# Memory attention in a decoder trunk: query and output weights multiplied with the memory's keys and values on chip

## The chip, the cores and the metric

The kernel runs on one core of a Trainium2 chip. The metric is the device time of one execution in microseconds (us), and lower is better. Engines are named as in the profile: PE is TensorE's matrix unit (PEld its weight load), DVE is VectorE, ACT is ScalarE, POOL is GpSimd, SP is SyncE, which here only starts DMA transfers.

## The reference, cut to what matters

One layer is applied to a prompt of 2048 tokens and to 8 separate decode tokens. A mixer (a gated convolution beside an mLSTM with 4 heads) is followed by attention over 256 memory rows and a SwiGLU feed-forward part; all of it is fp32. What the change touches is the attention:

```python
def mem_kv(mem, g_mem, w_xkv):
    kk, vv = jnp.split(rmsnorm(mem, g_mem) @ w_xkv, 2, axis=-1)
...
def cross_attn(xn, mk, mv, w_xq, w_xo):
    q = (xn @ w_xq).reshape(B, T, X_HEADS, X_HEAD_DIM)      # 4 heads of 256
    s = jnp.einsum('bthd,bmhd->bhtm', q, mk) * (X_HEAD_DIM ** -0.5)
    p = jax.nn.softmax(s, axis=-1)
    o = jnp.einsum('bhtm,bmhd->bthd', p, mv).reshape(B, T, X_HEADS * X_HEAD_DIM)
    return o @ w_xo
...
hp = hp + cross_attn(rmsnorm(hp, g_cross), pk, pv, w_xq, w_xo)             # prompt: its own memory
hs = hs + cross_attn(rmsnorm(hs, g_cross), cache_mem_k, cache_mem_v, ...)  # decode: cached keys, values
```

The memory keys and values of the prompt (pk, pv) are outputs as well.

## The kernel before

**Blocks.** The prompt is cut into five blocks of 4, 3, 3, 3 and 3 chunks of 128 tokens (`BLK`), that is one block 512 tokens wide and four 384 wide. The 8 decode tokens ride as 8 more columns: through the mixer with block 1 (`DM`), through the output projection and the query projection with block 2 (`DO`), through attention's output projection and the feed-forward part with block 3 (`DX`).

**Groups.** All weights are cut into groups of [128, 1024], that is 8 tiles of 128x128. `gemm` (L487) runs one group: for each of the 8 tiles three matmuls, since each fp32 operand is split in a high and a low part (hi x hi, hi x lo, lo x hi), with the weights stationary and the tokens moving; all of them stand on line 503. First come 16 groups for the memory's keys and values (`G_KV`), 256 columns wide. Then each block has 121 groups: 1 for the gates, 4 for `sg`, 24 for the heads of the mixer, 8 for its output (OUT), 8 for the queries (XQ), 8 for attention's output (XO), and 68 for the feed-forward part in three rounds. A stage can be found in the trace by counting matmuls of line 503: 24 make a group (fewer in the last two rounds of the feed-forward part), 384 the memory's part, 2856 a block.

**Weights.** A group's split weights lie in one of `NS` = 5 slots of `w_hl`. In block 0 a group comes from HBM as raw fp32 into one of two `w_raw` buffers, ACT makes the high part (`w_high`, L812), POOL the low part (L407; DVE does it for the 16 groups of the memory, L1164), and SP stores both to `split_d` in HBM (`keep`, 1 MB). In the later blocks SP loads the 1 MB of the split group (`split`, L344) as soon as the slot's last user is done. SP's queue is in order.

**Attention, before.** After `opening` (L653), which runs two XQ groups and a sum of squares for the norm, the XQ groups go on; DVE scales each result by the norm (`query`, L1441), ACT and DVE split it in high and low. Between the gemm steps, by hooks at fixed places, PE runs per head: `scores` (L662; 6 matmuls of 256 columns for each chunk, line 671), `ptrans` (L676; transposes of the probabilities, line 681) and `pv` (L684; 4 plain fp32 products as wide as the block, line 688). DVE takes maxima and normalises, ACT exponentiates, and both move results between them. The XO groups run interleaved with the last two heads. Plain fp32 products stand in the trace as two matmul records each.

**Around it.** In the mixer's heads PE runs per chunk `t_part` (transposes, keys by queries) and `n_part` (products with the state) from hooks between gemm steps, each at a place of its own. In block 0, `turn_mem` transposes the memory's values (16 transposes, line 537) in the `sg` stage. Decode attention runs on DVE in the feed-forward part of block 2 in 32 pieces (`dec_piece`) at the places of `PIECE_AT`; their rows and caches are loaded from POOL's queue (`decode_caches`). PE has `NP` = 3 banks for gemm results, so it can be two groups ahead of the engine that reads them.

## Time and profile before

| | us |
|---|---|
| median of 3 runs | 2981.76 (2981.4 to 2985.2) |
| the profiled execution, its own time | 2983.26 |
| its span, first to last instruction | 2981.4 |
| PE busy in the span | 2932.7 (98%) |
| DVE, ACT, POOL busy | 1212.0, 762.6, 378.2 |
| memory's 16 groups (9.09 to 73.55) | 64.46 |
| XQ and XO of block 0 (317.01 to 437.71) | 120.70 |
| XQ and XO of block 4 (2603.07 to 2692.61) | 89.54 |

Matmuls overlap in the pipeline, so the mean length of one record is longer than the time from one start to the next; a stage's own length, divided by its matmuls, gives that time. A time of a stretch holds waits as well as work. The mean granted clock of TensorE is 0.995 of full speed, and the DMA engines move 260 GB/s on average.

### The profile page before, as it was taken

What the parts mean: (1) busy time and instruction counts of PE and PEld (TensorE: products, weight loads), DVE (VectorE), ACT (ScalarE), POOL (GpSimd) and SP (SyncE); (2) the same over time, 40 slices, a digit from 0 to 9 for tenths busy, and PEclk for the clock granted to TensorE, in tenths of its full rate; (3) what the DMA queues carried; (4) which work ended last, traced back from release to release, by engine and by line L of the source; (5) the groups of instructions that cost most, each with busy time, mean ns of one, the idle gap of its engine ahead of it and who ended that gap; (6) DMA issues with size and microseconds to landing.
All of it is one profiled execution on the core that took longest, in us unless ns stands there. A gap on an engine that the chain in (4) does not pass through costs nothing.

```text
span 2981.4 us, 39316 instructions
## 1 busy us (share of the span) xinstructions
PE 2932.7 (98%) x16212; PEld 2771.1 (93%) x16212; DVE 1212.0 (41%) x2327; ACT 762.6 (26%) x1510; POOL 378.2 (13%) x251
## 2 busy tenths in 40 slices
PE   7999999999999999999999999999999999999998
PEld 7778778888899999999999999999999999999998
DVE  6355554234624344233344546334322243442223
ACT  4433433232332220113232011322311032231001
POOL 0443434444210000000000111000000000000000
PEclk9999999999999999999999999999999999999999
DMA  5876858789776498777667989866467777647775
GB/s 198 318 261 221 281 199 302 267 283 317 283 279 245 159 328 301 267 265 282 216 227 269 339 323 370 304 225 251 170 242 260 261 258 274 227 176 250 254 268 193
DMA packets 126873, 776.11 MB, mean 260 GB/s; under 512 B 15172, under 2 KB 18692, under 8 KB 46952
## 3 DMA queue, kind: packets, MB, share of 16 engines
q1 hardware_dynamic: 109840, 710.78, 65.7%
q0 software_dynamic: 13904, 59.48, 5.9%
q10 hardware_dynamic: 2952, 3.34, 0.4%
q8 instruction: 130, 2.13, 0.3%
q14 instruction: 47, 0.39, 0.0%
HBM read 633.59 MB, written 139.95 MB: 259 GB/s over the span
## 4 chain that ended last, share of the span: by engine, by line
PE 89%; DMA 4%; DVE 2%; ACT 2%; POOL 1%; issue 1%; SPq 0%; ACTq 0%; DVEq 0%
PE gb L503 82%; DMA w_raw<-w_st 2%; PE ta L671 2%; POOL w_hl L407 1%; DMA w_hl<-split_d 1%; PE tb L688 1%; PE td L688 1%; ACT w_hl L812 1%; DMA w_raw<-w_kv 1%; PE ta L592 0%; DVE w_hl L1164 0%; PE ta L511 0%; PE tb L561 0%; PE gm L681 0%; PE tb L603 0%
## 5 line engine op out<-in xcount | busy, mean ns | idle before, releaser
L503 PE MATMUL gb<-xn_hi,w_hl 128*128 128x384 f32 (+2 forms) x6480 | 1795.7, 351 | 10.7 <-DVE xn_lo L1159 4.3
L503 PEld LDWEIGHTS gb<-xn_hi,w_hl 128*128 128x128 f32 x6480 | 1188.5, 188 | 70.8 <-DMA w_hl<-split_d 5.8
L503 PE MATMUL gb<-xn_lo,w_hl 128*128 128x384 f32 (+2 forms) x3240 | 1124.3, 347 | 0.0
L503 PE MATMUL gb<-act_hi,w_hl 128*128 128x384 f32 (+3 forms) x3296 | 874.3, 344 | 17.3 <-DVE w_hl L1164 10.7
L503 PEld LDWEIGHTS gb<-act_hi,w_hl 128*128 128x128 f32 x3296 | 599.3, 189 | 44.9 <-DVE w_hl L1164 11.0
L503 PEld LDWEIGHTS gb<-xn_lo,w_hl 128*128 128x128 f32 x3240 | 610.4, 188 | 29.0 <-issue 1.4
L503 PE MATMUL gb<-act_lo,w_hl 128*128 128x384 f32 (+3 forms) x1648 | 564.1, 342 | 0.0
L1207 DVE TENSOR_TENSOR work<-gb,r_res 128x384 f32<-128x384 f32 (+2 forms) x260 | 151.7, 585 | 633.4 <-PE gb L503 570.4
L407 POOL TENSOR_TENSOR w_hl<-w_raw,w_hl 128x1024 fp32r<-128x1024 f32 x121 | 294.6, 2439 | 484.8 <-ACT w_hl L812 484.8
L503 PEld LDWEIGHTS gb<-act_lo,w_hl 128*128 128x128 f32 x1648 | 311.9, 189 | 13.4 <-issue 0.7
L1393 DVE TENSOR_TENSOR x<-x,gb 128x384 f32<-128x384 f32 (+2 forms) x200 | 115.3, 581 | 374.6 <-PE gb L503 371.9
L812 ACT ACTIVATE w_hl<-w_raw 128x1024 fp32r<-128x1024 f32 x132 | 138.9, 1057 | 323.5 <-DMA w_raw<-w_st 160.4
L1069 ACT ACTIVATE work<-work 128x384 f32<-128x384 f32 (+2 forms) x110 | 59.9, 545 | 504.6 <-DVE work L1207 504.5
L1072 ACT ACTIVATE act_hi<-work 128x384 fp32r<-128x384 f32 (+2 forms) x110 | 60.0, 546 | 345.5 <-DVE work L1620 345.5
L986 ACT ACTIVATE work<-x 128x384 f32<-128x384 f32 (+2 forms) x120 | 65.5, 546 | 270.1 <-DVE x L1393 249.8
L1403 DVE TENSOR_TENSOR r_res<-r_res,work 128x384 f32<-128x384 f32 (+2 forms) x120 | 94.6, 788 | 69.2 <-ACT work L986 67.7
L1620 DVE TENSOR_TENSOR work<-work 128x384 f32<-128x384 f32 (+2 forms) x110 | 86.6, 787 | 30.7 <-ACT work L1069 20.5
L876 ACT ACTIVATE big<-gb,cst 128x384 f32<-128x384 f32 (+1 forms) x80 | 48.6, 608 | 197.0 <-PE gb L503 196.8
L378 POOL DMA_DIRECT2D big<-rows_d x20 | 10.9, 550 | 684.4 <-DMA rows_d<-big 684.4
L1607 DVE TENSOR_TENSOR act_lo<-work,act_hi 128x384 fp32r<-128x384 f32 (+2 forms) x110 | 85.6, 778 | 14.5 <-ACT act_hi L1072 13.9
L1303 DVE TENSOR_TENSOR work<-ta,big 128x128 f32<-128x128 f32 x64 | 18.6, 291 | 150.4 <-ACT work L957 150.4
L1406 DVE SCALAR_TENSOR_TENSOR xn_lo<-x,cst,xn_hi 128x384 fp32r<-128x384 f32 (+2 forms) x80 | 55.8, 697 | 0.0
(246 smaller groups left out, 1809.0 us busy)
## 6 DMA issues: line engine op xcount, KB each, us to landing
w_hl<-split_d SPq DMA_DIRECT2D x484, 1024.0 KB, 5.1
split_d<-w_hl SPq DMA_DIRECT2D x121, 1024.0 KB, 5.0
w_raw<-w_st SPq DMA_DIRECT2D x121, 512.0 KB, 5.9
w_raw<-w_kv SPq DMA_DIRECT2D x16, 512.0 KB, 3.4
big<-kd_d POOLq DMA_DIRECT2D x8, 1024.0 KB, 8.4
big<-vd_d POOLq DMA_DIRECT2D x8, 1024.0 KB, 11.4
x<-x_blk POOLq DMA_DIRECT2D x8, 768.0 KB, 8.9
big<-x_blk POOLq DMA_DIRECT2D x6, 768.0 KB, 6.1
```

The costliest lines, as they stand in the source:

```text
L407: pool.tensor_tensor(w_lo[:, g % NS, :], w_raw[:, g % NR, :], w_hi[:, g % NS, :].bitcast(F32), ALU.subtract).then_inc(w_lo_done, 1)
L503: mm = pe.matmul(gb[:, ps, 0:wd], a[:, s, k * P:(k + 1) * P], r[:, k, 0:wd], start=(first and k == ks[0] and i == 0), stop=(last and k == ...
L671: mm = pe.matmul(ta[:, t // 2, (t % 2) * 256:(t % 2) * 256 + 256], a[:, kt, t * P:(t + 1) * P], r[:, kt, :], start=(dt == 0 and i == 0), s ...
L812: act.activation(w_hi[:, n % NS, :], w_raw[:, n % NR, :], ACT.Copy).then_inc(w_hi_done, 1)
L986: act.activation(sq_res[:, 0:wd], x[:, e, 0:wd], ACT.Square).then_inc(res_sq, 1)
L1069: act.activation(et[:, 0:W], gt[:, 0:W], ACT.Silu).then_inc(e_ffn, 1)
L1072: act.activation(act_hi[:, f, 0:W], ht[:, 0:W], ACT.Copy).then_inc(hid_hi, 1)
L1207: return lambda ps: v.tensor_tensor(dst[:, 0:wd], ps[:, 0:wd], r_res[:, 0:wd], ALU.mult)
L1393: return lambda ps: v.tensor_tensor(x[:, e, 0:wd], x[:, e, 0:wd], ps[:, 0:wd], ALU.add)
L1403: v.tensor_tensor(acc_res[:, 0:wd], acc_res[:, 0:wd], sq_res[:, 0:wd], ALU.add).then_inc(res_acc, 1)
L1607: v.tensor_tensor(act_lo[:, f, 0:W], ht[:, 0:W], act_hi[:, f, 0:W].bitcast(F32), ALU.subtract).then_inc(hid_lo, 1)
L1620: v.tensor_tensor(ht[:, 0:W], et[:, 0:W], ut[:, 0:W], ALU.mult).then_inc(h_ffn, 1)
```

## The change

For each head, scores are xn (Wq Kt), and the attention's output is P (V Wo). The change makes both products once, after the memory's groups, and stores them into `split_d` at the places of the XQ and XO groups, which then hold 1024 x 1024 products instead of weights:

- 32 products (`NPRE`): 16 for the keys (12 matmuls of 256 columns each), 16 for the values (6 of 512). ACT and DVE split each in high and low into a ring of four buffers (`made`), and ACT stores it in two DMA transfers. The weights come as 16 more raw groups (`G_MEM` = 16, `G_KV` = 32). The norm of block 0's input (`next_scale`, `next_high`, `next_low`) moves from the memory's groups into this stage.
- In every block, XQ becomes `wide`: tokens are stationary, the product moves with 512 columns, and the scores of two heads for a chunk come out by token in one bank. The norm is one number per token and is applied in the exponent's scale. `scores`, `pv`, `query` and the copies between them go; XO runs on the probabilities' transposes. Groups of XQ and XO are not loaded raw in block 0 but as split groups, by a loop on SP.
- The decode tokens no longer ride in XQ and XO. Their query and output projections are plain fp32 products of 8 stationary columns and 512 moving ones: 16 between the XO groups of block 2 (`decode_queries`), 16 between the OUT groups of block 3 (`decode_outputs`), with rows of `w_xq` and `w_xo` loaded from POOL's queue (`decode_rows`), and 8 small transposes.
- `NS` is 6. `turn_mem` goes. In the heads, `t_part` and `n_part` share hooks. The 32 pieces of decode attention keep their number and start two places later.

```diff
-G_KV = 16
+G_MEM = 16
+G_KV = 32
+NPRE = 32
-NS = 5
+NS = 6
-PIECE_AT = [2 * f + 1 for f in range(1, 8)] + [16 + m for m in (0, 1, 2, 4, 5, 6)] + [G1 + 2 * f + 1 for f in range(3)]
+PIECE_AT = [2 * f + 1 for f in range(3, 8)] + [16 + m for m in range(8)] + [G1 + 2 * f + 1 for f in range(3)]
...
+def raw(g):
+    return g < G_LOW and not attends(g)
...
-        mem_k_hi = sb("mem_k_hi", [P, KT, NMEM], F32R)
-        mem_k_lo = sb("mem_k_lo", [P, KT, NMEM], F32R)
-        mem_v = sb("mem_v", [P, MT, D])
+        dwt = sb("dwt", [P, 4, D])
...
+                if g == gw(0, O_OUT + KT - 1):
+                    for made_stored in pre_stored:
+                        sp.wait_ge(made_stored, 8 * NPRE)
+                    for a in range(gw(0, O_XQ), gw(0, O_FF[0])):
+                        kept(sp, a - NS)
+                        split(a)
...
+            def decode_rows(i):
+                after(pool, dw_used, i - 3)
+                pool.dma_start(dwt[:, i % 4, :], w_dec[i] if i < KT else w_kv[G_MEM + i]).then_inc(dw_loaded[i % 4], 16)
...
+            for h in range(HEADS):
+                pe.wait_ge(mem_lo, 2 * h + 2)
+                for j in range(4):
+                    i = h * 4 + j
+                    bank = pre_bank(i)
+                    for n in range(2):
+                        for dt in range(2):
+                            g = G_MEM + 2 * h + dt
+                            if j == 0 and n == 0:
+                                slot_ready(g)
+                            c = (2 * j + n) * P
+                            for f, (a, r) in enumerate([(w_hi, act_hi), (w_hi, act_lo), (w_lo, act_hi)]):
+                                mm = pe.matmul(bank[:, n * NMEM:(n + 1) * NMEM], a[:, g % NS, c:c + P], r[:, 2 * h + dt, NMEM:2 * NMEM],
+                                               start=(dt == 0 and f == 0), stop=(dt == 1 and f == 2))
+                    if j < 3:
+                        mm.then_inc(pre_done, 1)
+                    else:
+                        mm.then_inc(group_done, 2)
+            for h in range(HEADS):
+                pe.wait_ge(mem_lo, KT + 2 * h + 2)
+                for j in range(4):
+                    i = HEADS * 4 + h * 4 + j
+                    bank = pre_bank(i)
+                    mt, half = j // 2, j % 2
+                    for dt in range(2):
+                        g = G_MEM + KT + 2 * h + dt
+                        if j == 0:
+                            slot_ready(g)
+                        for f, (a, r) in enumerate([(act_hi, w_hi), (act_lo, w_hi), (act_hi, w_lo)]):
+                            mm = pe.matmul(bank, a[:, 2 * h + dt, mt * P:(mt + 1) * P], r[:, g % NS, half * 512:half * 512 + 512],
+                                           start=(dt == 0 and f == 0), stop=(dt == 1 and f == 2))
+                    if j < 3:
+                        mm.then_inc(pre_done, 1)
+                    else:
+                        mm.then_inc(group_done, 2)
...
-                    if b == 0:
-                        hooks[6] = lambda: turn_mem(h)
...
+                    c_hooks = {2: lambda: t_part(h, 0), 6: lambda: t_part(h, 1) or n_part(h, 0)}
                     if CH == 3:
-                        c_hooks = {2: lambda: t_part(h, 0), 4: lambda: t_part(h, 1), 7: lambda: n_part(h, 0)}
-                        h_hooks = {1: lambda: t_part(h, 2), 3: lambda: n_part(h, 1), 7: lambda: n_part(h, 2)}
+                        h_hooks = {2: lambda: t_part(h, 2) or n_part(h, 1), 7: lambda: n_part(h, 2)}
                         b_hooks = None
                     else:
-                        c_hooks = {2: lambda: t_part(h, 0), 4: lambda: t_part(h, 1), 6: lambda: n_part(h, 0)}
-                        h_hooks = {0: lambda: t_part(h, 2), 2: lambda: n_part(h, 1), 4: lambda: t_part(h, 3), 6: lambda: n_part(h, 2)}
+                        h_hooks = {1: lambda: t_part(h, 2) or n_part(h, 1), 5: lambda: t_part(h, 3) or n_part(h, 2)}
                         b_hooks = {1: lambda: n_part(h, 3)}
...
+                def decode_outputs(m):
+                    if m == 3:
+                        pe.wait_ge(do_ready, 2 * NDEC)
+                    for i in (2 * (m - 3), 2 * (m - 3) + 1):
+                        pe.wait_ge(dw_loaded[i % 4], 16 * ((KT + i) // 4) + 16)
+                        for half, bank in enumerate((ta[:, 1, :], td)):
+                            mm = pe.matmul(bank[0:NDEC, :], dy[:, i * NDEC:(i + 1) * NDEC], dwt[:, i % 4, half * 512:half * 512 + 512],
+                                           start=i == 0, stop=i == KT - 1)
+                        mm.then_inc(dw_used, 1)
+                def turn_outputs():
+                    pe.wait_ge(qrow_done, 4)
+                    for i in range(KT):
+                        mm = pe.matmul(tb[:, i * NDEC:(i + 1) * NDEC], dwt[0:NDEC, 0, i * P:(i + 1) * P], ident[0:NDEC, 0:NDEC],
+                                       start=True, stop=True)
+                    mm.then_inc(dox_t, 1)
...
+                def sum_cols():
+                    pe.wait_ge(res_acc, b * 27 + 9)
                     for t in range(CH):
-                        for dt in range(2):
-                            kt = 2 * h + dt
-                            for i, (a, r) in enumerate([(act_hi, mem_k_hi), (act_lo, mem_k_hi), (act_hi, mem_k_lo)]):
-                                mm = pe.matmul(ta[:, t // 2, (t % 2) * 256:(t % 2) * 256 + 256], a[:, kt, t * P:(t + 1) * P],
-                                               r[:, kt, :], start=(dt == 0 and i == 0), stop=(dt == 1 and i == 2))
-                        if t % 2 or t == CH - 1:
...
+                def wide(p, hooks):
+                    for q in range(4):
+                        g = gw(b, O_XQ) + 4 * p + q
+                        slot_ready(g)
                         for t in range(CH):
-                            m = pe.transpose(bank[:, t * P:(t + 1) * P], prob[:, t, mt * P:(mt + 1) * P], ident)
-                        m.then_inc(pt_done, 1)
+                            for n in range(2):
+                                kt = 2 * q + n
+                                if p == 0 and t == 0:
+                                    pe.wait_ge(res_lo, b * 16 + kt + 1)
+                                for f, (a, r) in enumerate([(xn_hi, w_hi), (xn_lo, w_hi), (xn_hi, w_lo)]):
+                                    mm = pe.matmul(score_bank(p, t), a[:, kt, t * P:(t + 1) * P], r[:, g % NS, n * 512:n * 512 + 512],
+                                                   start=(kt == 0 and f == 0), stop=(kt == KT - 1 and f == 2))
+                            if t == CH - 1:
+                                mm.then_inc(group_done, 1)
+                            elif q == 3:
+                                mm.then_inc(s_done, 1)
+                            if (q, t) in hooks:
+                                hooks[q, t]()
+                wide(0, {(1, CH - 1): sum_cols})
+                    wide(1, {(1, 2): lambda: ptrans(0, 0) or ptrans(0, 1), (2, 2): lambda: ptrans(1, 0) or ptrans(1, 1)})
...
+                def decode_queries(m):
+                    if m == 3:
+                        pe.wait_ge(dxq_ready, 1)
+                        pe.wait_ge(exp_done, ch0(b + 1))
+                    for i in (2 * (m - 3), 2 * (m - 3) + 1):
+                        decode_product(i, i, dxq[:, i, :], (ta[:, 1, :], td))
...
-                    gemm(gw(b, O_XO + i), W, act_hi, act_lo, (2 * h, 2 * h + 1), None if i else o_wait,
+                    gemm(gw(b, O_XO + i), TOK, act_hi, act_lo, (2 * h, 2 * h + 1), None if i else o_wait,
                          first=h == 0, last=h == HEADS - 1)
                 xo(0, 0)
-                ptrans(2)
                 xo(1, 0)
-                scores(3)
                 xo(2, 0)
-                pv(2)
                 xo(0, 1)
+                ptrans(2, 0)
+                ptrans(2, 1)
                 xo(1, 1)
-                ptrans(3)
-                xo(0, 2)
-                xo(1, 2)
-                pv(3)
                 xo(2, 1)
-                xo(2, 2)
-                for i in range(3):
-                    xo(i, 3)
+                ptrans(3, 0)
+                ptrans(3, 1)
+                for h in (2, 3):
+                    for i in range(3):
+                        xo(i, h)
...
+            def store_made(i):
+                act.wait_ge(pre_lo, i + 1)
+                h, j = (i // 4) % HEADS, i % 4
+                for s in range(2):
+                    if i < NPRE // 2:
+                        dst = split_d[O_XQ + 4 * (h // 2) + j, :, s, :].rearrange("p (n h m) -> p n h m", n=2, h=2)[:, :, h % 2, :]
+                        act.dma_start(dst, made[:, i % 4, s, :].rearrange("p (n m) -> p n m", n=2)).then_inc(pre_stored[i % 4], 16)
+                    else:
+                        kt, m0 = 2 * h + j // 2, O_XO + j % 2 * 4
+                        dst = split_d[m0:m0 + 4, :, s, kt * P:(kt + 1) * P].rearrange("m p c -> p m c")
+                        act.dma_start(dst, made[:, i % 4, s, :].rearrange("p (m c) -> p m c", m=4)).then_inc(pre_stored[i % 4], 16)
+            for i in range(NPRE):
+                pre_made(act, i)
+                after(act, pre_stored[i % 4], 32 * (i // 4))
+                act.activation(made[:, i % 4, 0, :].bitcast(F32R), gb[:, (G_MEM + i) % NP, :], ACT.Copy).then_inc(pre_hi, 1)
+                if i:
+                    store_made(i - 1)
+                if i % 4 == 3:
+                    w_high(G_MEM + i // 4 * 2)
+                    w_high(G_MEM + i // 4 * 2 + 1)
+                if i < KT:
+                    read_out(act, G_MEM - 1)
+                    act.activation(act_hi[:, i, 0:NMEM], vfeat[:, i, :], ACT.Copy).then_inc(mem_hi, 1)
+                elif i < 2 * KT:
+                    next_high(0, i - KT)
+            store_made(NPRE - 1)
...
+            for i in range(NPRE):
+                v.wait_ge(pre_hi, i + 1)
+                v.tensor_tensor(made[:, i % 4, 1, :].bitcast(F32R), gb[:, (G_MEM + i) % NP, :], made[:, i % 4, 0, :],
+                                ALU.subtract).then_inc(pre_lo, 1)
+                if i < KT:
+                    v.wait_ge(mem_hi, KT + i + 1)
+                    v.tensor_tensor(act_lo[:, i, 0:NMEM], vfeat[:, i, :], act_hi[:, i, 0:NMEM].bitcast(F32),
+                                    ALU.subtract).then_inc(mem_lo, 1)
+                    next_scale(0, i)
+                elif i < 2 * KT:
+                    next_low(0, i - KT)
...
+                def maxima(p, t):
+                    if t < CH - 1:
+                        v.wait_ge(s_done, ch0(b) // 2 - 2 * b + p * (CH - 1) + t + 1)
+                    else:
+                        v.wait_ge(group_done, gw(b, O_XQ) + 4 * p + 4)
+                    st(v.tensor_reduce(mx[:, t, :, 0], score_bank(p, t).rearrange("p (h m) -> p h m", h=2), AX.X, ALU.max))
+                    st.settle()
+                    v.tensor_scalar(mx[:, t, :, 1], mx[:, t, :, 0], r_neg[:, t:t + 1], None, ALU.mult).then_inc(mx_done, 1)
+                def normalise(p, t):
+                    v.wait_ge(exp_done, ch0(b, 2 * p) + 2 * t + 2)
+                    st(v.reciprocal(mx[:, t, :, 3], mx[:, t, :, 2]))
+                    st.settle()
+                    for i in range(2):
+                        v.tensor_scalar(prob[:, t, i, :], prob[:, t, i, :], mx[:, t, i, 3:4], None, ALU.mult).then_inc(p_done, 1)
+                for p in range(2):
+                    maxima(p, 0)
+                    for t in range(1, CH):
+                        maxima(p, t)
+                        normalise(p, t - 1)
+                    normalise(p, CH - 1)
+                    prob_low(2 * p)
+                    prob_low(2 * p + 1)
```

## Rows read from the trace of the kernel before

**Rows 1.** The page, part 1: PE's busy time, share of the span, instructions.
```profile
PE 2932.7 (98%) x16212; PEld 2771.1 (93%) x16212; DVE 1212.0 (41%) x2327; ACT 762.6 (26%) x1510; POOL 378.2 (13%) x251
```

**Rows 2.** The chain in order of time: start us, length us, what, instructions.
```profile
385.61 2.87 PE ta L671 x24
...
449.34 161.88 PE gb L503 x714
...
2700.70 267.32 PE gb L503 x1542
```

**Rows 3.** Stretches: from:to, length, each engine's busy us, clock, DMA share, GB/s.
```profile
9.09:73.55 64.46, 54.41 (x389) 51.44 (x389) 46.34 (x67) 33.12 (x50) 5.57 (x2) 0.95 0.57 189
73.55:86.27 12.72, 8.42 (x25) 6.05 (x25) 8.73 (x11) 5.83 (x11) 5.08 (x3) 0.78 0.92 347
86.27:112.94 26.67, 26.67 (x116) 21.54 (x115) 11.55 (x14) 11.70 (x19) 12.01 (x5) 0.91 0.88 323
...
317.01:381.82 64.81, 62.38 (x299) 49.57 (x298) 36.06 (x61) 27.25 (x54) 22.98 (x11) 1.00 0.77 266
381.82:437.71 55.89, 55.37 (x250) 43.53 (x248) 29.52 (x38) 21.24 (x36) 17.22 (x7) 1.00 0.49 174
...
2603.07:2649.97 46.90, 46.90 (x278) 44.44 (x278) 19.57 (x51) 13.96 (x37) 0.00 (x0) 1.00 0.49 181
2649.97:2692.61 42.64, 42.17 (x239) 39.70 (x239) 17.97 (x38) 12.94 (x29) 0.00 (x0) 1.00 0.53 195
...
1793.34:1856.61 63.27, 60.55 (x336) 58.06 (x337) 45.67 (x67) 6.84 (x13) 7.91 (x12) 1.00 1.01 393
```

**Rows 4.** Timeline, PE: start, length, what; plain fp32 products, 512 columns.
```profile
375.66 1.88 PE L688 MATMUL td<-big,mem_v 128*128 128x512 f32 x4
377.37 1.88 PE L688 MATMUL tb<-big,mem_v 128*128 128x512 f32 x4
```

**Rows 5.** Timeline, PE: the first two gemm matmuls behind an `n_part`.
```profile
901.23 0.43 PE L503 MATMUL gb<-xn_hi,w_hl 128*128 128x392 f32 x1
901.49 0.35 PE L503 MATMUL gb<-xn_lo,w_hl 128*128 128x392 f32 x1
```

**Rows 6.** Groups by form, ACT: busy us, mean ns, idle before and its releasers.
```profile
L812 ACT ACTIVATE w_hl<-w_raw 128x1024 fp32r<-128x1024 f32 x132 | 138.9, 1057 | 323.5 <-DMA w_raw<-w_st 160.4 <-issue 111.4 <-PE gb L503 46.1
...
L829 ACT ACTIVATE xn_hi<-big 128x512 fp32r<-128x512 f32 x8 | 5.0, 629 | 9.3 <-DVE big L1153 9.3
...
L1012 ACT ACTIVATE act_hi<-tb 128x512 fp32r<-128x512 f32 x4 | 2.4, 600 | 4.5 <-PE tb L688 4.5
```

**Rows 7.** Timeline, ACT: its sequencer starting one DMA transfer.
```profile
28.03 0.45 ACTq L847 DMA_DIRECT2D dec<-st_m  x1
```

**Rows 8.** Waits of ACT from 66 to 440 us: total us, times, longest.
```profile
ACT w_hl L812 <- DMA w_raw<-w_st: 37.7, 16, 4.4
```

**Rows 9.** One stretch, columns as in group 3; SP's and ACT's queues both move.
```profile
20.00:28.00 8.00, 6.52 (x36) 6.17 (x36) 4.37 (x9) 3.67 (x10) 0.00 (x0) 0.63 0.92 351
```

**Rows 10.** DMA issues: queue, count, KB each, median us to landing.
```profile
x<-mem_x ACTq DMA_DIRECT2D x4, 256.0 KB, 7.9
...
o_mv<-work SPq DMA_DIRECT2D x1, 1024.0 KB, 9.6
```

**Rows 11.** Groups by form, the softmax on ACT and DVE.
```profile
L1000 ACT ACTIVATE work<-ta,work 128x256 f32<-128x256 f32 x64 | 29.6, 471 | 48.7 <-DVE work L1425 48.7
...
L1000 ACT ACTIVATION_READ_ACCUMULATOR work<-ta,work 128x1 f32 x64 | 12.8, 200 | 0.0
...
L1433 DVE TENSOR_SCALAR work<-work 128x256 f32<-128x256 f32 x64 | 22.6, 354 | 2.3
...
L1422 DVE TENSOR_REDUCE work<-ta 128x2 f32<-128x512 f32 x24 | 16.6, 690 | 24.9 <-PE ta L671 24.9
```

**Rows 12.** Groups by form: POOL's low parts; DVE reading a 512-column bank.
```profile
L407 POOL TENSOR_TENSOR w_hl<-w_raw,w_hl 128x1024 fp32r<-128x1024 f32 x121 | 294.6, 2439 | 484.8 <-ACT w_hl L812 484.8
...
L1207 DVE TENSOR_TENSOR work<-gb,r_res 128x512 f32<-128x512 f32 x52 | 35.8, 689 | 117.6 <-PE gb L503 111.2 <-ACT r_res L819 6.4
```

453 lines of the change are left out of this document (232 added, 221 removed).

## The prediction

> **What bounds the kernel now.** I read the page first: PE is busy for 98% of the span and no other engine for half of it [rows 1]. So only PE's time counts, as work or as gaps, and I cost every edit there. The chain in order of time gives PE's prices, because long runs of one line have no gap in them: 714 matmuls of 512 columns in 161.88 us are 226.7 ns each, 1542 of 384 in 267.32 are 173.4, 24 score matmuls of 256 in 2.87 are 119.6 [rows 2]. I then cut the span by counting matmuls of line 503 and read the stretches. Attention takes 89.5 us in block 4 and 120.7 in block 0 [rows 3]; the pairs of blocks 1, 2 and 3 are three more like block 4's, within 0.8 us. Of 89.5 us, 384 gemm matmuls are 66.6. The first stretches are the other place to look: the memory's groups take 64.5 us with PE busy for 54.4, the gate group behind them 12.7 us, and there the clock and the DMA share (0.92) show a stage that isn't PE's alone [rows 3].
>
> **Attention, blocks 1 to 4.** Scores go: 72 matmuls at 119.6 ns, 8.6 us. The products with the values go: two plain fp32 products of 512 columns start 1.71 us apart from the next two [rows 4], so one is 857 ns; at 384 columns it is 643, and 16 are 10.3 us. XQ's 192 matmuls of 384 columns (33.3 us) become 144 of 512 (32.6): 0.7 less. XO and the transposes stay. Each change from small products back to gemm costs 0.26 us where 0.177 is usual [rows 5], some 0.085 more; thirteen insertions become five, 0.7 less. New is one wait. The softmax of the second pair of heads starts when `wide(1)` ends, and PE has only four XO pieces (24 matmuls, 4.2 us) to cover it. Its last chunk needs a maximum 0.7, two exponents with their sums 2 x 0.67, two scalings 2 x 0.35 [rows 11], and about 1.7 for the normalising of the chunk before it, small operations and signals (an estimate): 4.5 us. So 0.4 us stays open; the first pair has 8.2 us of `wide(1)` over it and costs nothing. Sum: 8.6 + 10.3 + 0.7 + 0.7 - 0.4 = 19.9 us a block, **79.6** for four.
>
> **Attention, block 0.** Scores 96 x 119.6 = 11.5, values 16 x 857 = 13.7, insertions 0.7. Besides, of 120.7 us about 116.6 are work by the same prices, and of the 4 us of gaps I let 2.8 go, since its groups come split and ACT and POOL no longer have to split them in time. **28.7**.
>
> **The new stage.** PE needs 16 x 12 x 119.6 + 16 x 6 x 226.7 ns = 44.7 us, but it isn't PE that sets it. ACT does, per product, a copy out of the bank (600 ns) and two DMA starts (450 each) [rows 6, 7], and over the stage 16 weight copies of 1057 ns and 16 further copies of up to 629 [rows 6]: 19.2 + 28.8 + 16.9 + 10.1 = 75 us. DVE has 32 x 0.69 and the moved norm, POOL 16 x 2.44 = 39 us [rows 12]; both are under that. DMA moves 16.8 MB of products, 5.2 MB of weights and, behind them on SP's queue, some 6.3 MB of the next groups; at 351 GB/s for a share of 0.92 [rows 9] that is 74 us. Two engines so evenly loaded don't overlap fully: ACT waits for a raw weight, and all products queue behind it. Block 0 shows 16 such waits of 2.4 us [rows 8]; ten weights are still to come, and I let seven or eight of them wait: 18. I take 75 + 18 = 93 us. The bounds: 74 if nothing waits; above, the ring of four buffers. A product's buffer is free when its store has landed, issued one product later, so a period of (landing + 1.5) / 3. ACT's 256 KB loads at the start landed in 7.9 us, a 1 MB store in 9.6 [rows 10]: 3.1 to 3.7 us a product, 100 to 118 us. The memory's groups lose the moved norm (3 us of gaps by the stretch's end), and the gate group finds its weights and its norm ready: 6 us for 12.7. From 9.09 to the end of the gate group that is 61.4 + 93 + 6 = 160.4 for 77.2: **83.2 more**.
>
> At TensorE's lower clock level (1.2 GHz, not 2.4), which the stretch around the start shows after PE had waited there (0.63 mean [rows 9]), the 32 products would take PE 89 us, still under 93. So the clock doesn't set this stage; it can add up to 5 us to the gate group behind it, and that is in the range.
>
> **The other parts.** `sg`: 26.7 us [rows 3] less 21.8 for its 96 matmuls and 0.9 for the picked row leave 4.0 for `turn_mem` and the lower clock: **4.0** gained. Shared hooks: two insertions fewer per head and 384-wide block, three in block 0, at 0.085: 3.7, less a doubt about new waits for DVE: **3.5**. Decode: 32 plain products of 512 columns at 857 ns, 27.4, and 1.6 for eight small transposes and ACT's copies in front of them: **29.0 more**; the 8 columns saved in XQ and XO are 0.6 and disappear in it. Its rows, 4 MB twice from POOL's queue, I cost at nothing: a row is asked for when its buffer is free and used two groups and three products later (some 10 us or more). If that cover is gone, PE stands for the rest of a landing, a few us in two blocks. The later pieces of decode attention cost nothing while PE can be two groups ahead. The sixth slot: in block 2's third feed-forward round 14 groups of 24 took 63.3 us where 336 x 173.4 ns is 58.3, with the DMA engines at a share of 1.01 [rows 3]; one more slot is 1 MB of lead, and I give it 3 of the 5 us, **3.0**. Its other effect, that each block's attention no longer gives DMA a rest (0.49 and 0.53 of the engines there, [rows 3]), I cost at nothing: the feed-forward groups ask the same rate without gaps.
>
> **Sum.** +83.2 - 4.0 - 3.5 - 28.7 - 79.6 + 29.0 - 3.0 = -6.6 us. The profiled execution took 2983.26 with a span of 2981.4, the median of three is 2981.76, so span and median are the same to 0.4 us and I take the sum from the median: **2975 us**.
>
> **The rivals.**
> 1. *The new stage runs at ACT's own pace.* Stores land early and weights are there: 74 us and not 93, 2956 us. For it: six weights are split ahead, and the 16 last products carry no norm. Against it: the shares of ACT and DMA, 75 and 74 us, leave no room. A rule stands on its side: the Trainium skill, DMA: Bandwidth & Descriptors, section "Anatomy of one DMA — SWDGE (gpsimd) path", gives about 2 us plus the bytes at 436 GB/s for one transfer (fitted for transfers from GpSimd). An estimate by it is 2.6 us for 256 KB, a ring that never waits, and so this rival's 2956; the 7.9 us of the row speak against it, and no row shows such a store alone. 0.22.
> 2. *The ring of stores sets the stage: slower.* Once a store takes longer than 7.2 us to land, the period passes the 2.9 us of my 93. At 9.6 it is 118, the whole 3000 us. For it: the landings seen, and pieces of 512 bytes to 1 KB. Against it: those landings were queued behind larger ones. 0.20.
> 3. *The softmax isn't covered.* PE has one place per block where nothing else can go. If ACT and DVE take 9 us and not 4.5, each block gives 5 back: 25 us, 3000. Against it: the waits before, with shorter covers, were 0.5 us. 0.08.
>
> **How the numbers follow.** My case has 0.50, with a range of 2964 to 2986 of its own. The range of 8 in 10 reaches into the rivals: 2952 to 3000. A measurement of this kernel can tell about 0.2%, 6 us, so "faster" is under 2976 and "slower" over 2988. Faster: about half of my case and all of rival 1, 0.48. Same: the rest of my case below 2988 and the mild end of rival 2, 0.25. Slower: 0.27.
>
> **What would show it.** Right: block 4's attention at 69 to 70 us; 72 records of scores and 32 of values gone; block 0's at 92; a stretch of about 93 us between the last memory group and the gate group in which ACT is busy for most of the time, counting its DMA starts, and waits for raw weights; OUT of block 3 and XO of block 2 longer by 14 us each; block 2's third round near 60. Wrong: a stage under 80 or over 105 us; PE waiting for probabilities by more than 1 us a block; plain products of 8 rows at another price than 857 ns; gaps of PE behind DMA in blocks 1 to 4, which would mean that the rest in attention was needed; heads longer than before.

## The result, and the profile after

| | before | after |
|---|---|---|
| median of 5 runs, us | 2981.76 (2979.66 to 2985.2) | 2999.5 (2996.88 to 3001.9) |
| the profiled execution, its span, us | 2981.4 | 2999.2 |
| mean granted clock | 0.995 | 0.991 |

The changed kernel is slower by 17.7 us: the ratio is 1.0058, with a 95% interval of 1.0045 to 1.007. The forecast was 2975, within 2952 to 3000, and "slower" had a chance of 0.27. PE is less busy than before by 15 us, against [rows 1], in a span that is 18 us longer. So the change removed work from PE, as forecast, and put more than twice as much waiting in its place.

The page of the changed kernel, part 1:

```profile
PE 2917.5 (97%) x15851; PEld 2728.0 (91%) x15851; DVE 1171.4 (39%) x2249; ACT 745.1 (25%) x1470; POOL 386.3 (13%) x267
```

The stages were cut by counting gemm matmuls, as for [rows 3], with the same columns (from:to, length, busy us of PE, PEld, DVE, ACT, POOL, clock, DMA share, GB/s). In order: the memory's groups, the products of the keys, those of the values, the gate group, `sg`, block 0's heads; block 0's scores and XO; block 2's XO, its second and third feed-forward rounds; block 3's OUT; block 4's scores and XO.

```profile
9.33:77.05 67.72, 55.87 (x389) 53.07 (x389) 42.27 (x58) 32.73 (x50) 7.21 (x3) 1.00 0.55 178
77.05:122.23 45.18, 28.75 (x193) 27.01 (x193) 36.57 (x41) 22.69 (x40) 22.05 (x9) 0.89 0.76 255
122.23:168.56 46.33, 29.66 (x96) 21.31 (x97) 14.36 (x22) 18.73 (x27) 19.29 (x8) 0.81 1.02 324
168.56:175.67 7.11, 7.11 (x25) 5.73 (x25) 0.93 (x2) 1.06 (x1) 1.39 (x1) 0.77 1.02 379
175.67:198.33 22.66, 22.66 (x100) 18.40 (x98) 5.60 (x10) 6.83 (x10) 8.20 (x4) 1.00 0.96 356
198.33:369.67 171.34, 160.85 (x774) 134.38 (x772) 75.22 (x143) 67.23 (x131) 64.63 (x31) 0.96 0.73 258
413.65:459.95 46.30, 46.30 (x217) 38.50 (x216) 12.70 (x32) 9.19 (x25) 0.00 (x0) 1.00 0.52 183
459.95:506.29 46.34, 45.57 (x209) 37.62 (x208) 29.74 (x44) 20.19 (x39) 12.44 (x5) 1.00 0.59 212
1596.09:1645.72 49.63, 49.63 (x237) 36.98 (x236) 16.94 (x36) 11.20 (x26) 3.18 (x6) 1.00 0.68 254
1746.54:1808.62 62.08, 59.68 (x342) 58.74 (x341) 29.59 (x43) 10.96 (x19) 4.43 (x7) 1.00 0.84 320
1837.74:1897.66 59.92, 59.17 (x338) 58.08 (x337) 44.95 (x67) 6.83 (x13) 10.03 (x16) 1.00 1.02 401
2065.65:2116.34 50.69, 50.69 (x244) 37.81 (x244) 15.79 (x30) 9.23 (x18) 3.65 (x6) 1.00 0.66 239
2640.49:2675.23 34.74, 34.74 (x163) 28.92 (x163) 10.91 (x30) 8.22 (x25) 0.00 (x0) 1.00 0.69 244
2675.23:2709.90 34.67, 34.67 (x206) 34.59 (x205) 16.95 (x36) 11.22 (x26) 0.00 (x0) 1.00 0.65 239
```

Most of the forecast stands here as it was made: block 4's attention takes 69.4 us, block 0's 92.6, the products 91.5. The row to look at is the sixth. It is a stage whose weights and products the change doesn't touch; I had only let it gain a little by the shared hooks. Before, it was this, in the kernel before, same view:

```profile
112.94:273.02 160.08, 155.87 (x773) 130.06 (x772) 76.02 (x143) 63.06 (x126) 60.07 (x29) 0.99 0.74 260
```

It is 11.3 us longer, PE is idle for 10.5 us in it (4.2 before), and its clock is 0.96. The table sets each term of the sum beside what was measured (stage after less stage before, in us; a minus is a gain).

| term | forecast | measured |
|---|---|---|
| memory's groups | -3.1 | +3.3 |
| the products | +93 | +91.5 |
| gate group | -6.7 | -5.6 |
| `sg` | -4.0 | -4.0 |
| heads, all blocks | -3.5 | +11.4 |
| attention, block 0 | -28.7 | -28.1 |
| attention, blocks 1 to 4 | -79.6 | -81.7 |
| decode products | +29.0 | +32.0 |
| sixth slot, block 2's third round | -3.0 | -3.4 |
| later pieces, block 2's second round | 0 | +2.9 |
| sum | -6.6 | +18.3 |

The difference to +17.7 lies in small changes of other stages. The forecast missed by 24.3 us: 14.9 of it in the heads, 6.4 in the memory's groups, 3.0 in the decode products, 2.9 in the pieces; the other stages give 2.9 back. The waits of PE in block 0's heads (engine, tile and line waited for: us, times, longest), in the kernel before and then in the changed one, and the changed kernel's clock there, in stretches of 6 us:

```profile
PE tb L603 <- DVE work L1304: 4.2, 3, 2.1
```
```profile
PE tb L708 <- DVE work L1498: 6.3, 4, 2.4
PE tb L672 <- ACT big L1106: 4.2, 1, 4.2
```
```profile
204.30:210.30 6.00, 3.98 (x13) 3.53 (x14) 0.00 (x0) 4.39 (x7) 1.38 (x3) 0.64 0.57 187
210.30:216.30 6.00, 6.00 (x20) 5.02 (x19) 1.13 (x2) 4.45 (x4) 5.63 (x4) 0.51 0.89 306
216.30:222.30 6.00, 6.00 (x28) 4.95 (x27) 0.20 (x1) 1.75 (x2) 1.19 (x1) 1.00 0.92 345
```

PE stands for 4.2 us (to 206.3), and then TensorE runs at its lower level (1.2 GHz, 0.51 of the 2.4) until 216: of the PE time in the first two of these stretches, 3.98 x 0.36 + 6.00 x 0.49 = 4.4 us are lost to that, by this estimate. With 4.2 for the wait and 2.1 for longer waits at line 708 (6.3, at line 603 before 4.2) this is 10.7 of the 11.3. What PE waits for is the exponents of the gates' rows. ACT's timeline (start, length, what, idle before it):

```profile
203.94 1.06 ACT L969 ACTIVATE w_hl<-w_raw 128x1024 fp32r<-128x1024 f32 x1 [4.02 <-issue]
204.90 0.61 ACT L1101 ACTIVATE big<-big 128x512 f32<-128x512 f32 x1
...
206.06 0.21 ACT L1106 ACTIVATE big<-big 128x4 f32<-128x4 f32 x1
```

By DVE's timeline their input was ready at 193.3. They ran at 204.9: ACT's queue is in order, and three weight copies of block 0 stand ahead of them, which ACT reached at 194.3, 198.3 and 203.9 after standing for 6.1, 2.4 and 4.0 us. By the program each waits for its turn in the loop of load, high part, low part and store. My theory was that the opening leaves ACT's queue behind in that loop. The rivals were the shared hooks, and a plain lack of DMA bandwidth.

### The profile page after: what moved, and what is told of

Read it like the earlier page. It is cut to its first block, busy times and chain, and to the rows that moved or that the text cites. A ratio compares the mean times of both kernels' runs of the same rounds, so it can differ in the third digit from the quotient of the medians.

```text
span 2999.2 us, 38561 instructions
## 1 busy us (share of the span) xinstructions
PE 2917.5 (97%) x15851; PEld 2728.0 (91%) x15851; DVE 1171.4 (39%) x2249; ACT 745.1 (25%) x1470; POOL 386.3 (13%) x267
## 4 chain that ended last, share of the span: by engine, by line
PE 87%; DMA 5%; DVE 2%; ACT 2%; POOL 1%; issue 1%; ACTq 1%; SPq 0%; DVEq 0%
PE gb L580 76%; PE gb L828 3%; DMA w_raw<-w_st 2%; PE ta L828 2%; DMA w_raw<-w_kv 1%; POOL w_hl L460 1%; ACT w_hl L969 1%; PE td L828 1%; DMA big<-kd_d 1%; ACTq L1048 1%; DMA w_hl<-split_d 1%; PE ta L697 0%; PE gm L810 0%; PE tb L708 0%; DVE work L1498 0%
## 5 line engine op out<-in xcount | busy, mean ns | idle before, releaser
L580 PE MATMUL gb<-xn_hi,w_hl 128*128 128x384 f32 (+2 forms) x5840 | 1598.7, 350 | 5.3 <-issue 2.2
L580 PEld LDWEIGHTS gb<-xn_hi,w_hl 128*128 128x128 f32 x5840 | 1070.7, 188 | 56.4 <-issue 6.6
L580 PE MATMUL gb<-xn_lo,w_hl 128*128 128x384 f32 (+2 forms) x2920 | 1013.5, 347 | 0.0
L580 PE MATMUL gb<-act_hi,w_hl 128*128 128x384 f32 (+3 forms) x3296 | 872.2, 344 | 20.9 <-DVE w_hl L1352 11.3
L580 PEld LDWEIGHTS gb<-xn_lo,w_hl 128*128 128x128 f32 x2920 | 550.0, 188 | 25.3 <-issue 0.7
L1402 DVE TENSOR_TENSOR work<-gb,r_res 128x384 f32<-128x384 f32 (+2 forms) x220 | 128.3, 585 | 554.6 <-PE gb L580 518.4
L1599 DVE TENSOR_TENSOR r_res<-r_res,work 128x384 f32<-128x384 f32 (+2 forms) x120 | 81.4, 678 | 56.5 <-ACT work L1187 54.9
L429 POOL DMA_DIRECT2D big<-rows_d x20 | 10.9, 552 | 667.5 <-DMA rows_d<-big 667.5
L828 PE MATMUL gb<-w_hl,xn_hi 128*128 128x512 f32 x240 | 76.5, 392 | 0.0
```

The costliest lines, as they stand in the source:

```text
L580: mm = pe.matmul(gb[:, ps, 0:wd], a[:, s, k * P:(k + 1) * P], r[:, k, 0:wd], start=(first and k == ks[0] and i == 0), stop=(last and k == ...
L828: mm = pe.matmul(score_bank(p, t), a[:, kt, t * P:(t + 1) * P], r[:, g % NS, n * 512:n * 512 + 512], start=(kt == 0 and f == 0), stop=(kt ...
L1402: return lambda ps: v.tensor_tensor(dst[:, 0:wd], ps[:, 0:wd], r_res[:, 0:wd], ALU.mult)
L1599: v.tensor_tensor(acc_res[:, 0:wd], acc_res[:, 0:wd], sq_res[:, 0:wd], ALU.add).then_inc(res_acc, 1)
```

## The experiments

Each run is compared with runs of the kernel before on the same chip. Stages are cut as above, and a ratio without more words is to the kernel before.

**The order of ACT's queue.**

```diff
-                for h in range(HEADS):
-                    if h == HEADS - 1:
+                def row_exps():
                         act.wait_ge(rows_pre, b + 1)
                         st(act.activation(row_g[:, 0:TOK], row_g[:, 0:TOK], ACT.Exp))
...
+                for h in range(HEADS):
+                    if h == (1 if b == 0 else HEADS - 1):
+                        row_exps()
                     take(gw(b, O_SIG + h), sg[:, h, :], dk_o[:, h * NDEC:(h + 1) * NDEC], bias=col(C_BIN + 7 * h + 3))
                     w_high(gw(b, O_SIG + h))
```

> One order is changed, in block 0 alone: on ACT the two exponents of the gates' rows (lines 1101 and 1102) and the copy behind them stand ahead of the second `sg` group's result instead of the fourth's, so that two more weight copies (line 969) don't stand in front of them. Theory A: block 0's heads are 11.3 us longer in the changed kernel because ACT's in-order queue holds these exponents behind weight copies that wait for a store (the copy ahead of them waited 4.0 us, DVE's rows had been ready at 193.4, the exponents ran at 204.9), PE waits 4.2 us for them and then runs at half the clock for some 8 us. Then the 4.2 us wait goes, the clock stays at full level after it, the heads fall from 171.3 to 161 to 164 us, and the whole from 2999.5 to 2989 to 2992. Rival B: the weights are late by themselves (ACT, POOL and SP's stores split them at 5 us a group), and the wait only moves to a gemm group: heads stay at 169 to 172, the whole at 2998 to 3000, with a new wait of PE for a low part or a store. Rival C: the shared hooks cost it: unchanged as well, but with the 6.3 us of waits at line 708 as they are.

2996.8 us, ratio 1.0051 (1.0036 to 1.0066). The heads fell from 171.3 to 165.2, at a clock of 0.99; they and the whole lie between theory A's figures and rival B's. PE's waits in them, in this run:

```profile
PE tb L708 <- DVE work L1501: 5.5, 4, 1.6
PE ta L695 <- ACT big L1078: 3.7, 1, 3.7
```

The wait for the exponents is gone. A new one stands at line 695, where the transposes of the first head wait for ACT to read a head's gemm result, which stood behind the next weight copies. So theory A named the place rightly, and rival B is nearer the cause: ACT is late with the weights by itself, and what stands behind them in its queue is late in turn. PE's waits fell by only 1.3 us, its busy time by 4.8: the clock didn't fall as deep, and that is most of the gain.

**The hooks.**

```diff
-                    c_hooks = {2: lambda: t_part(h, 0), 6: lambda: t_part(h, 1) or n_part(h, 0)}
...
-                        h_hooks = {2: lambda: t_part(h, 2) or n_part(h, 1), 7: lambda: n_part(h, 2)}
+                        c_hooks = {2: lambda: t_part(h, 0), 4: lambda: t_part(h, 1), 7: lambda: n_part(h, 0)}
+                        h_hooks = {1: lambda: t_part(h, 2), 3: lambda: n_part(h, 1), 7: lambda: n_part(h, 2)}
```

> The changed kernel with the hooks of before: each `t_part` and `n_part` of the heads at a place of its own. Theory of the prediction: a return from small products to the gemm costs 0.085 us, so that the heads of blocks 1 to 4 grow by 0.7 us each and the whole by 3.5. Theory A: sharing hooks gained nothing (blocks 1 to 4 stand at 118.6, 116.7, 116.7, 116.7 before and after), so these stay within 0.2 us. For block 0's heads: if the shared hooks cause PE's four waits for DVE at line 708 (6.3 us, where before had three of 4.2 us), these fall back to about 4 us and the heads from 171.3 to 169; if block 0's 11 us come from the hooks altogether, they fall to 160. Theory A gives 2997 to 2999.5 for the whole, the prediction's 3003.

2999.75 us, ratio 1.0058 (1.0043 to 1.0073). The heads of blocks 1 to 4 agree with those of the changed kernel to 0.25 us, block 0's are 170.2. Sharing hooks gains nothing, and it isn't what made block 0 longer.

**The sixth weight at the start.** With six slots ACT and DVE split six raw weights between the first tiles of the memory. Here the sixth comes behind the eighth tile; `first_high` holds ACT's two lines that were in the loop.

```diff
-                if k < NS:
-                    act.wait_ge(w_loaded[k % NR], 16 * (k // NR) + 16)
-                    act.activation(w_hi[:, k, :], w_raw[:, k % NR, :], ACT.Copy).then_inc(w_hi_done, 1)
+                if k < 5:
+                    first_high(k)
...
+                if k == KT - 1:
+                    first_high(5)
...
-                if k < NS:
+                if k < 5:
                     w_low(k)
...
+                if k == KT - 1:
+                    w_low(5)
```

> The changed kernel, but the high and low part of the sixth raw weight are made behind the eighth tile of the memory's own preparation instead of between the sixth and the seventh. Theory A: the sixth slot puts one more raw weight, which arrives late, into ACT's and DVE's queues ahead of the last tiles of the memory; that is the wait of 5.8 us before PE's seventh tile (24.2 to 30.0 us) that the kernel before doesn't have, and the memory's stage is 67.7 us for 64.5 by it. Then the wait goes, the memory's stage falls to 62 to 64 us, and the whole by 4 to 5.5 us to 2994 to 2995.5. Rival B: the stage is set by the landing of raw weights at 512 KB each (some 3 us), whatever the order; the wait goes to the third group, and the stage stays at 66.5 to 68 us. Rival C: the stage falls, but the stage of the 32 products behind it takes it back, because its weights come no earlier: the stretch to the end of the products stays at 159 us.

2993.0 us, ratio 1.0039 (1.0025 to 1.0054). The memory's groups fell from 67.7 to 60.6 us, and the products behind them took nothing back (45.2 and 46.2). PE's wait for the memory's tiles, in the changed kernel and then in this run:

```profile
PE gb L580 <- DVE act_lo L1327: 9.2, 4, 5.8
```
```profile
PE gb L580 <- DVE act_lo L1333: 4.0, 3, 1.9
```

Theory A holds: the sixth slot cost 7.1 us there, since the sixth raw weight came late and the last two tiles of the memory waited behind it on two in-order engines.

**Five slots.**

```diff
-NS = 6
+NS = 5
```

> The changed kernel with five weight slots instead of six. Theory A: the sixth slot costs 7 us at the start (as the run with the sixth weight's parts later showed: 67.7 to 60.6) and gives back 3.3 us in block 2's third feed-forward round (63.3 before, 59.9 after): then the memory's stage is 60 to 62 us, that round 63 to 63.5, block 0's heads within 2 us of 171.3, the whole 2994 to 2997. Rival B: the sixth slot also carries the products and block 0's heads through the crowded DMA queues: keys and values together 94 to 98 us for 91.5, heads 173 to 178, the whole 3003 to 3010.

2989.3 us, ratio 1.0028 (1.0017 to 1.0039): 8.8 us over its own runs of the kernel before, where six slots were 17.7 over theirs, so 9 us are gained. Memory's groups, the products of the values, block 0's heads, block 2's second round (its second half) and third round:

```profile
9.45:70.20 60.75, 55.04 (x388) 52.72 (x389) 40.24 (x58) 31.43 (x48) 4.80 (x2) 1.00 0.57 192
115.67:164.35 48.68, 28.93 (x96) 21.26 (x97) 15.93 (x22) 18.67 (x27) 18.86 (x8) 0.80 1.00 322
194.42:355.19 160.77, 154.53 (x774) 129.26 (x773) 75.16 (x143) 65.36 (x129) 63.06 (x31) 1.00 0.74 265
1793.61:1824.94 31.33, 30.05 (x169) 28.86 (x168) 18.56 (x27) 0.53 (x1) 6.03 (x10) 1.00 0.97 370
1824.94:1885.86 60.92, 59.73 (x337) 58.17 (x338) 43.21 (x64) 6.84 (x13) 9.13 (x15) 1.00 1.02 402
```

The slot's use in block 2 is there, 2.2 us (31.3 for 29.1) and 1.0, together near the 3.0 that I gave it. But block 0's heads are at 160.8, which neither theory had. So 10.6 of the 11.3 us in the heads go with the sixth slot. How is read from the program and ACT's timelines, and not tested by itself: at each place in its queue ACT then makes the weight five groups ahead and not six, and it stood 9.5 us ahead of the three copies before the exponents, 12.5 with six. The values' half took 2.3 us of the gain back.

**The order of SP's queue.** `keep` waits for the low part and issues the store of 1 MB, `weights` the load of 512 KB.

```diff
                 else:
-                    keep(g)
+                    sp.wait_ge(w_lo_done, RAW[g] - G_MEM)
                 if i < len(raws):
                     weights(raws[i])
...
+                if g >= G_KV:
+                    keep(g)
```

> The changed kernel, but on SP's queue, in block 0, the load of the next raw group (512 KB) is issued ahead of the store of the split group (1 MB) that waits for the same low part, not behind it. Bytes and waits are the same. Theory A: block 0's weights are a loop of load, ACT's high part, POOL's low part with two buffers, and its longest piece is the landing of the load (7.0 us in the opening, 3.3 where nothing is ahead of it in the queue); ACT's in-order queue waits in it, and the gates' rows, the head's copies and PE's 10.5 us of waits in block 0's heads follow from that. Then the landing falls to 4 us or so, the heads from 171.3 to 161 to 165, the whole to 2990 to 2994. Rival B: the bytes set it (share 0.95 to 1.1 from 122 to 198 us): what the load gains, the store loses, and the high part of the group six later waits for that store; heads 169 to 172, the whole 2998 to 3001.

2988.5 us, ratio 1.0024 (1.0015 to 1.0033). The gate group took 5.5 us for 7.1. The heads, and PE's waits in them:

```profile
196.79:357.13 160.34, 157.09 (x773) 131.54 (x772) 73.50 (x143) 66.42 (x131) 64.83 (x31) 0.98 0.77 276
```
```profile
PE tb L674 <- ACT big L1108: 2.3, 1, 2.3
PE tb L710 <- DVE work L1500: 1.0, 1, 1.0
```

The heads' 11 us come back with six slots too, with the same bytes, only because a load of 512 KB doesn't stand behind a store of 1 MB. So the loss goes with either of the two, the sixth slot or this order, and a plain lack of bandwidth isn't its cause. The landing of the loads behind 168 us fell less than expected (median 6.3 to 5.6 us); what counted is when they were issued and what they stood behind.

**The products.** Here the forecast's size was right (93 for 91.5), and the question is whether its reason was. It said that ACT sets the stage, two DMA starts a product among its costs.

```diff
-                for s in range(2):
-                    if i < NPRE // 2:
...
-                        act.dma_start(dst, made[:, i % 4, s, :].rearrange("p (n m) -> p n m", n=2)).then_inc(pre_stored[i % 4], 16)
...
+                if i < NPRE // 2:
...
+                    act.dma_start(dst, made[:, i % 4].rearrange("p s (n m) -> p s n m", n=2)).then_inc(pre_stored[i % 4], 16)
```

> The changed kernel, but each of the 32 products is stored by one DMA start of 512 KB instead of two of 256 KB, with the same bytes in the same pieces (1 KB for the keys, 512 bytes for the values). Theory A, as predicted: ACT's own time sets the products, and one start is 0.45 us or more of it; 32 fewer starts give 14 us, keys 45.2 to 38, values 46.3 to 39, the whole 2985. Rival B: in the values' half the DMA engines are full (share 1.02), and ACT's long starts (up to 5 us) only wait for room; in the keys' half DVE is held up (an operation of 0.74 us took 2.8 while POOL made low parts), and ACT waits for DVE. Then fewer starts give next to nothing: keys 43 to 45, values 45 to 47, the whole 2996 to 3000. In between: a start of twice the bytes takes twice as long, then the records of ACT's queue show about 0.9 us per start and nothing is gained either.

2995.1 us, ratio 1.0043 (1.0028 to 1.0058). Keys and values, and one row of ACT's timeline:

```profile
76.64:119.86 43.22, 28.70 (x193) 26.99 (x193) 36.46 (x41) 22.83 (x40) 22.07 (x9) 0.88 0.81 265
119.86:169.57 49.71, 27.69 (x96) 20.75 (x97) 13.73 (x22) 18.88 (x27) 19.36 (x8) 0.77 1.04 345
```
```profile
146.79 7.26 ACTq L1047 DMA_DIRECT2D split_d<-big  x1
```

Half of the starts are gone, the rest take 31 us of ACT's sequencer in all for 49 in the changed kernel, and yet the two halves together take 92.9 us. Where DMA is full (share 1.04) a single start lasts 7.3 us, and in the values' half ACT now waits for stores to land before it may fill their buffers again:

```profile
ACT big L1052 <- DMA split_d<-big: 13.5, 5, 7.3
```

So theory A, which is the forecast's reason, falls: much of the time that the starts no longer take returns as waits for the same bytes. Only the keys, where DMA is not full, gained 2.0 us. The heads of this run were at 164.6, 7 us shorter, with nothing changed in them; how late ACT's queue is there depends on how the opening ends.

The next run takes POOL's low parts out of the stage.

```diff
-            for g in range(G_MEM, G_LOW):
+            for g in range(G_KV, G_LOW):
                 if not raw(g):
                     continue
...
-                if g + NS < G_MEM:
-                    w_low(g + NS)
+                w_low(g + NS)
...
+                if i % 4 == 3:
+                    for g in (G_MEM + i // 4 * 2 + NS, G_MEM + i // 4 * 2 + 1 + NS):
+                        if g < G_KV:
+                            w_low(g)
```

The first loop is POOL's, the others are DVE's.

> The changed kernel, but the low parts of the 16 raw groups of the products are made by DVE (1.23 us each where it does it for the memory's groups) and not by POOL (2.44). Theory A: in the keys' half the period of a head (11.3 us for four products) is POOL's two low parts (4.9 us) and DVE's operations on the memory's values and the norm, which stretch while POOL works (0.41 to 1.44 us, 0.74 to 2.82) and which ACT and PE then wait for (PE's waits of 5.1, 4.2 and 1.9 us). Then no DVE operation there is longer than 0.8 us, a head takes some 9 us and the keys 45.2 to 36 to 39; the values' half, where the DMA engines are full (share 1.02), takes part of it back. Rival B: DMA's bytes set the whole opening: keys 38, values 52, sum unchanged at 91.5. Rival C: DVE has no time for it: keys 45 or more. The whole: A 2991 to 2995, B and C 2999.

2992.4 us, ratio 1.0038 (1.0024 to 1.0052): keys 36.8 us, values 50.0, heads 165.3. The keys:

```profile
76.25:113.06 36.81, 27.78 (x194) 26.29 (x193) 31.41 (x49) 22.00 (x39) 0.00 (x0) 0.91 0.88 294
```

What had held the keys is in the changed kernel's longest wait of PE there, in its timelines of POOL and of DVE, and in this run's group for the same DVE operation (line 1341, here 1339):

```profile
PE gb L627 <- DVE big L1382: 12.0, 4, 5.1
```
```profile
92.96 4.85 POOL L460 TENSOR_TENSOR w_hl<-w_raw,w_hl 128x1024 fp32r<-128x1024 f32 x2 [6.49 <-ACT w_hl L969]
```
```profile
94.17 1.44 DVE L1386 TENSOR_TENSOR act_lo<-work,act_hi 128x256 fp32r<-128x256 f32 x1 [2.00 <-ACT act_hi L1061]
95.54 2.82 DVE L1341 SCALAR_TENSOR_TENSOR big<-big,cst,r_mix 128x512 f32<-128x512 f32 x1
98.28 0.68 DVE L1382 TENSOR_TENSOR big<-gb,big 128x512 fp32r<-128x512 f32 x1
```
```profile
L1339 DVE SCALAR_TENSOR_TENSOR big<-big,cst,r_mix 128x512 f32<-128x512 f32 x8 | 6.0, 744 | 0.0
```

While POOL makes two low parts (92.96 to 97.81), DVE's operations with two operands on chip (in SBUF) end only after POOL's have ended: 2.82 us for what takes 0.74. The low part of the product behind them (line 1382), which PE waits for, comes 2 us late or more. With POOL out of the stage the eight take 744 ns in the mean, and the keys are 8.4 us shorter, as theory A had it. DVE also makes a low part faster than POOL does (1.2 us for 2.4), but no wait of PE in the keys' half was for POOL, so that isn't what the keys gained by. The Trainium skill, SBUF — State Buffer, section "SBUF: two separate sides", says that these two engines share one pair of ports as an exclusive lock, held for a whole instruction, and that a DVE operation with two SBUF inputs needs it against a GpSimd operation that reads SBUF; the trace agrees (2.82 us for 0.74). Line 1382, which reads one operand from a bank of results, was not held: two of them at 128.7, while POOL worked from 125.8 to 131.0, took 0.64 each. The values' half took 3.7 us of the gain back.

The next run halves the products' bytes.

```diff
-                for s in range(2):
+                for s in range(1):
...
-                sp.dma_start(w_hl[:, g % NS].bitcast(F32), split_d[(g - G_KV) % G_BLK]).then_inc(split_loaded[g % NS], 16)
+                s = slice(0, 1 if attends(g) else 2)
+                sp.dma_start(w_hl[:, g % NS, s].bitcast(F32), split_d[(g - G_KV) % G_BLK][:, s]).then_inc(split_loaded[g % NS], 16)
```

> The changed kernel with half of the products' bytes left out: their low parts are made but not stored, and the attention's groups load the high half alone (the low half that the products there use is whatever stands in the slot). So 8.4 MB less are stored in the opening, by 32 starts instead of 64, and 8 MB less are loaded in each block. Theory A: the values' half is set by DMA (share 1.02, 46.3 us; PE needs 21.8): then it falls to 32 to 38, the gate group and the first groups of the heads find their weights earlier, and block 0's heads fall from 171.3 to 160 to 165; the keys (share 0.76) stay at 42 to 45. The whole 2974 to 2982. Rival B: the round from PE to ACT to DVE and back sets both halves: keys 43 to 45, values 43 to 46, heads 170, the whole 2995 to 3000. Since one start instead of two of the same bytes gave nothing in an earlier run, the starts themselves explain at most 2 us of a difference.

2986.4 us, ratio 1.0021 (1.0011 to 1.003). Keys 43.0, and the values:

```profile
119.74:160.26 40.52, 26.18 (x96) 19.53 (x97) 14.38 (x22) 19.57 (x28) 19.43 (x8) 0.87 0.91 303
```

With half of the bytes the values take 40.5 us, less than 46.3 and more than the 32 to 38 of theory A, and the whole misses its 2974 to 2982. DMA's share is still 0.91, now with the raw weights and stores of block 0's own groups, which SP moves ahead of their use. So bytes are part of it. That the rest is ACT's queue, in which block 0's weights stand between the products, is tested further down. Block 0's heads fell to 163.2, within theory A's range: fewer bytes in the opening shorten them as well, so how full the DMA engines are has a share in that loss.

**All together.** Three of these edits don't concern each other: the sixth weight later, the low parts on DVE, the load ahead of the store.

> The changed kernel with three edits of the runs above at once: the sixth raw weight's parts behind the memory's eighth tile, the low parts of the products' raw groups on DVE, the load of the next raw group ahead of the store. If the three causes are separate, their stages add up: memory 60.6, keys 37, values 50, heads 160 to 161, the whole 2975 to 2979, faster than before by 0.1 to 0.2%. If the opening is one block of bytes for DMA (the values' half took 3.7 us back when the keys' half got 8.4 us shorter), every us saved ahead of it returns in the values, the gate group or the heads: the stretch from the memory's last group to the heads' end stays at 285 us or more, and the whole at 2982 to 2986.

2973.3 us, ratio 0.9973 (0.9962 to 0.9983): faster than before. Memory, keys, values and heads:

```profile
9.35:69.92 60.57, 53.70 (x389) 51.28 (x389) 40.43 (x62) 32.99 (x50) 0.00 (x0) 0.94 0.60 204
69.92:106.18 36.26, 27.81 (x194) 26.39 (x193) 31.56 (x49) 21.88 (x39) 0.00 (x0) 0.91 0.89 299
106.18:150.65 44.47, 28.38 (x99) 20.42 (x97) 18.56 (x26) 18.93 (x29) 9.36 (x4) 0.85 1.06 343
180.45:339.58 159.13, 154.15 (x773) 128.96 (x772) 73.02 (x143) 65.20 (x129) 63.79 (x31) 1.00 0.76 276
```

The gains add up: each beside its own runs of the kernel before, the three alone gained 6.7, 5.9 and 9.7 us, and together 25.6. From the memory's last group to the end of the heads it is 269.7 us for 292.6, so what is saved doesn't return as it would if the opening were one block of bytes. In the whole the three causes are separate; in the values' half they aren't, which takes 44.5 us where 50 was expected. The same without the sixth slot:

```diff
-NS = 6
+NS = 5
```

> The same with five slots (where the sixth weight doesn't exist, and so needs no place): low parts on DVE and the load ahead of the store. If the sixth slot is worth nothing beyond block 2's rounds (with five: second round's last part 31.3 for 29.1 us, third round 60.9 for 59.9), the time is that of the kernel with six and the three edits, plus 2 to 4 us: 2978 to 2982. If in the opening the sixth slot still pushes ACT's queue into waits, five slots are faster by 2 us or more.

2970.7 us, ratio 0.9965 (0.9952 to 0.9977): five slots are not slower here, and the intervals overlap. Block 0's heads:

```profile
183.64:337.02 153.38, 153.38 (x774) 129.04 (x772) 71.62 (x143) 63.09 (x125) 61.12 (x30) 1.00 0.76 275
```

PE has no gap left in them, at full clock: 153.4 us is their bare work, 6.7 us under the kernel before, and with six slots they are 5.8 us longer (159.1). So the sixth slot still costs the heads time with the load issued first. It gives that back elsewhere: with five the values' half is 2.7 us longer and block 2's feed-forward part 2.9. Then six slots again, with the memory's outputs stored earlier and the rows' exponents placed as in the first run:

```diff
-                if off == 6:
+                if off == G_MEM + 8 - G_KV:
                     read_out(sp, G_MEM - 1)
...
-                    if G_KV <= raws[i]:
-                        others(raws[i] - G_KV)
+                    others(raws[i] - G_KV)
```

> The kernel of the three edits, and besides the two 1 MB stores of the memory's keys and values are issued in the keys' half (in front of the raw group 8 places behind) and not behind block 0's seventh group, and the gates' rows' exponents stand ahead of the second `sg` result. Theory, DMA's bytes: 2 MB leave the values' half and the stretch behind it, in which DMA is full, and go to the keys' half (share 0.76 before): values 50 to 45 or 46, keys at most 2 us longer, the whole 2971 to 2976. Rival: the keys' half, shorter now, is full as well, and the stores only move: the whole within 1.5 us of the kernel of the three edits.

2972.7 us, ratio 0.9969 (0.9957 to 0.9982). The keys' half grew by 5.0 us, the values' by 2.3, the heads fell by 5.3: the whole stayed within 1 us of the kernel of the three edits. That is the rival's figure, 2 MB moved from one full stretch into another. But two edits were in this run, so what each of them gained or lost, and which of them shortened the heads, isn't told.

```diff
-PIECE_AT = [2 * f + 1 for f in range(3, 8)] + [16 + m for m in range(8)] + [G1 + 2 * f + 1 for f in range(3)]
+PIECE_AT = [2 * f + 1 for f in range(2, 8)] + [16 + m for m in (0, 1, 2, 4, 5, 6, 7)] + [G1 + 2 * f + 1 for f in range(3)]
```

> The same, and the 32 pieces of decode attention begin one place earlier and leave one gap among the eight places that follow (where the changed kernel puts eight in a row). Theory: block 2's second feed-forward round is 62.1 us for 59.2 before because a piece every 4.2 us comes faster than its 1 MB cache row lands (11 us for two pieces each), DVE waits 10.9 us for these rows and PE 2.4 for DVE; then that round falls to 59.2 to 60.5 and the whole by 1.5 to 3 us. Rival: the waits come from the rows' later start, which this doesn't change, or the first piece now waits for its row: no gain in that round, up to 1 us lost in the first.

2969.2 us, ratio 0.9959 (0.9947 to 0.9972), the lowest median of all, though its interval overlaps those of the three runs before it: 0.4% under the kernel before, and 1% under the changed kernel. Block 2's second round went from 62.1 to 59.2 us, and PE has no gap left in it:

```profile
1716.87:1776.03 59.16, 59.16 (x342) 58.80 (x341) 25.36 (x39) 10.96 (x19) 3.92 (x6) 1.00 0.85 321
```

**What was left open.** Two more runs, on the values' half and the sixth slot.

```diff
                 if i % 4 == 3:
-                    w_high(G_MEM + i // 4 * 2)
-                    w_high(G_MEM + i // 4 * 2 + 1)
+                    for g in (G_MEM + i // 4 * 2, G_MEM + i // 4 * 2 + 1):
+                        if g + NS <= G_KV:
+                            w_high(g)
...
             store_made(NPRE - 1)
+            for g in range(G_KV + 1 - NS, G_KV):
+                w_high(g)
```

> The kernel with all edits so far (pieces one place earlier among them), and besides ACT makes the high parts of block 0's own groups, but for the gate group, behind the last product and not between the products. Theory A, the order of ACT's queue: in the values' half ACT waits for raw weights that are wanted only two to six groups later (PE stood for 7.0 us before the last four products), and the products behind them wait as well; then the values' half falls from 44.8 to 36 to 40, the gate group and the `sg` groups take up to 3 us of it back, and the whole falls from 2969 to 2963 to 2967. Theory B, DMA's bytes: the engines are full there (share 1.02 to 1.06), so the values' half falls by 2 us at most, or what it gains returns as waits of PE in the gate group, `sg` and the heads: the whole 2968 to 2974.

2975.6 us, ratio 0.9981 (0.9972 to 0.999): slower than the version it was built on (0.9959). Values and `sg`, and PE's wait from 155 to 200 us:

```profile
111.54:151.26 39.72, 25.55 (x99) 18.22 (x97) 18.65 (x26) 16.20 (x26) 2.36 (x1) 0.89 1.06 334
159.03:193.69 34.66, 24.90 (x100) 19.49 (x98) 7.60 (x10) 12.82 (x17) 16.63 (x11) 0.85 0.88 317
```
```profile
PE td L660 <- ACT big L1091: 9.8, 1, 9.8
```

The values fell by 5.1 us, so ACT's order does hold them. But the gate group's result is now read behind five weight copies, PE waits 9.8 us for it, and `sg` grows by 12. Theory B named where the gain returns, though the whole came out above its range. The wait is where the weights stand in that queue, and moving them moves it. What the values' half would take with ACT's reads free of the weight loop wasn't tried.

The other is the version before it with `NS = 5` (and so without the sixth weight's place).

> The same kernel as f1 without its last edit, with five slots instead of six. Theory A: once the sixth weight no longer stands ahead of the memory's last tiles and the load ahead of the store, the sixth slot is worth what block 2 shows (59.9 for 62.7 us in its third round, 29.1 for 29.9 in the round before, 34.8 for 35.7 in block 3's scores): some 4 us, the whole 2972 to 2974. Theory B: what it saves there it costs in the opening, where one more group of 1.5 MB is moved ahead of its use: 2968 to 2970.

2971.6 us, ratio 0.9971 (0.9959 to 0.9983), against 0.9959 with six. Block 2 loses 4.4 us (31.5 for 29.1 and 62.2 for 60.1), the opening (from the memory's groups to the heads' end) gains 0.6. The places are theory A's; the whole lies between the two theories and the intervals overlap, so whether the sixth slot is worth some 2 us isn't settled.

## Why the prediction was wrong, by its steps

**The sixth slot.** This is the step that failed. It was costed as a gain of 3.0 us in block 2's third round, and its other effects, thought of only as DMA's rest in blocks 1 to 4, at nothing. In block 2 it gains that much (2.2 and 1.0 by the run with five), though mostly in the round before: of the third round's 3.4 us 2.4 stay with five slots, so that line of the table agrees in part by luck. What was in no term is the opening. The slot puts one more raw weight ahead of the memory's tiles (7.1 us, shown by the run that moved it and by the run with five), and in block 0 it makes ACT's in-order queue wait for each weight one group sooner, ahead of results that PE needs (10.6 us by five slots, and 5.8 between the two runs with the load issued first). With SP's load ahead of its store the 11 us go with six slots as well, so the slot and that order cause them together; that one group sooner is the way is read from the timelines and not tested by itself. [rows 8] had it in sight: in block 0 ACT had already waited 16 times for a raw weight. I used the row for the new stage, and not for the stage behind it.

The slot isn't the whole miss. With five slots the kernel is still 8.8 us slower than the kernel before, where the sum without the slot's 3.0 makes it 3.6 us faster. Of these 12.4 us the hooks (3.5), the decode products (3.0) and the pieces (2.9), each told below, are 9.4.

**Rival 2** gave the forecast's other side, by the ring of stores. It isn't what made this kernel slower: the 256 KB stores landed in 3.8 us (median of all, row below; 5.5 in the values' half), not in the 7.9 or 9.6 of [rows 10], no wait of ACT in the products is put down to a store's landing, and the products took 91.5 us. The ring does show once other costs are out of the way: 13.5 us of such waits with one start a product, 7.7 with block 0's weights behind the products. The Trainium skill, DMA: Bandwidth & Descriptors, section "Anatomy of one DMA — SWDGE (gpsimd) path", which gave 2.6 us by an estimate, was nearer to the 3.8 than my row. Yet rival 1 didn't follow from it, since landings were not what set the stage. The slower side came by a mechanism that I had not listed; that the measured 2999.5 lies just inside the range, near this rival's 3000, is luck. The row of the page's DMA issues after (queue, count, KB each, us to landing):

```profile
split_d<-big ACTq DMA_DIRECT2D x64, 256.0 KB, 3.8
```

**The new stage** was right in size (91.5 for 93) by luck, for a wrong reason. ACT is busy for 41 us of it, and halving its DMA starts shortened nothing in the whole. POOL's low parts, by the DVE operations that they hold up, cost the keys' half 8.4 us; in the values' half DMA's bytes (5.8 us by the run with half of them) and ACT's order (5.1) each hold part. ACT stood 18.3 us ahead of its weight copies, as much as the 18 that I let it wait for raw weights, but the trace puts only 7.9 of them down to a raw weight; for 8.8 it shows no cause but ACT's own queue, in which transfers were being started.

**The hooks** were worth nothing and not 3.5 us. The longer first matmul behind an insertion [rows 5] is not time that goes when an insertion goes; the run with the old hooks shows it.

**The pieces** were costed at nothing with PE two groups ahead as their cover. Eight in a row came faster than their cache rows landed (DVE waited 10.9 us for these rows, 7.0 before), and 2.9 us showed; beginning one place earlier, with one gap among them, gives it back.

**The decode products** cost 32.0 for 29.0. One product took 0.86 us, as [rows 4] said; the other 3.0 would lie in the four more insertions in each of two blocks and in the transposes, which no run took apart.

**Right:** the price of scores and values in attention: attention in blocks 1 to 4 to 2 us of 80, block 0's to 0.6 of 29, `sg`, the gate group to 1.1, rows for decode never late, and no wait for the softmax: PE has none over 0.8 us in attention. Rival 3 had no case. "Heads longer than before" stood among the signs of being wrong, and it came.

## What to carry to other kernels

One more buffer is also one more item in every in-order queue that fills it: count what stands behind that item on each engine, at the start and in each stage where the queue is late, before it is booked as a gain. On a queue of mixed loads and stores under one wait, issue the load that the next step needs first. When a new stage delays a loop of loads, look for the cost in the next stage that shares its queues, not in the new one alone.

## What the runs showed of the hardware

- DVE and POOL: an operation of 0.74 us with two operands on chip took 2.82 while POOL's two ran, and 0.74 in the mean of eight once POOL was idle; the keys' half got 8.4 us shorter with it, and the values' half 3.7 longer.
- A start of a DMA transfer on ACT's queue isn't a fixed cost: 0.45 us in [rows 7], 0.6 for 512 KB, and up to 7.3 where DMA's share was above 1. Half as many starts of twice the bytes saved nothing in the two halves together: 13.5 us of waits for stores to land came in their place.
- A wait of 4.2 us cost PE about as much again: the granted clock was at 0.64 in the stretch of 6 us in which it ended and at 0.51 in the next, by the estimate above 4.4 us of PE's time. A wait of 1.7 us there, in the run with five slots, left the heads' clock at 1.00.
